# Indexer scores: the keys' low part against the queries' high part alone, two heads in the two row halves of the array

## The reference, cut to what matters

```python
s_idx = jnp.einsum('bqhd,bsd->bqhs', qi_b, ki).astype(jnp.float32)
score = jnp.einsum('bqhs,bqh->bqs', jax.nn.relu(s_idx), wi_b.astype(jnp.float32))
causal = pos[None, None, :] <= pos_b[None, :, None]
score = jnp.where(causal, score, neg)
_, sel = lax.top_k(score, topk)          # topk = 256
```

## Time and profile before

| | |
|---|---|
| median of 3 executions | 1706.78 us (1706.37 to 1708.25) |
| profiled execution, span of the core | 1702.8 us (the page gives no other time of it) |
| TensorE busy | 97% of the span, 7403 matmuls |
| VectorE, ScalarE, GpSimd busy | 51%, 34%, 25% |
| chain of work that ended last | TensorE 86%, issue 7%, VectorE 3%, ScalarE 1% |
| granted TensorE clock in the scored tiles | 1.00 of full (the 2.4 GHz level) |

### The profile page before, as it was taken

The page is one execution under the profiler, slowest core; times in us unless marked ns, Lnnn a source line. Parts: engine busy times, 40 slices in busy tenths (PEclk is TensorE's granted clock), DMA queues, the critical chain, the costliest instruction groups (busy, mean ns, idle before and its releaser), DMA issues.

```text
span 1702.8 us, 21182 instructions
## 1 busy us (share of the span) xinstructions
PE 1655.7 (97%) x7403; PEld 1323.2 (78%) x7403; DVE 862.8 (51%) x1497; ACT 584.4 (34%) x849; POOL 420.7 (25%) x285
## 2 busy tenths in 40 slices
PE   5999999999999999999999999999998899999998
PEld 4777888888888888888888888877776788888886
DVE  6326445448678777787444444467677200022003
ACT  7234444444433344432111111155555222222330
POOL 1212111112222222222222222211010344444550
PEclk8999999999999999999999999999999999999999
DMA  7411111101222222223222222222122522227322
GB/s 257 82 38 54 52 31 37 37 13 53 65 65 65 59 59 59 59 74 103 70 74 68 74 72 69 75 78 80 59 81 76 208 91 95 98 87 296 116 95 99
DMA packets 132301, 141.35 MB, mean 83 GB/s; under 512 B 8510, under 2 KB 103840, under 8 KB 129952
## 3 DMA queue, kind: packets, MB, share of 16 engines
q1 hardware_dynamic: 130720, 136.55, 25.7%
q0 software_dynamic: 1536, 4.20, 0.8%
HBM read 116.08 MB, written 24.64 MB: 83 GB/s over the span
## 4 chain that ended last, share of the span: by engine, by line
PE 86%; issue 7%; DVE 3%; ACT 1%; DMA 1%; POOL 0%; DVEq 0%; SPq 0%; ACTq 0%; POOLq 0%
PE ps L1009 18%; PE ps L1011 18%; PE ps L1010 18%; PE ps L1269 6%; PE ps L1271 6%; PE ps L1270 6%; PE ps L1096 2%; PE ps L1098 2%; PE ps L1210 2%; PE ps L1174 1%; PE ps L1187 1%; PE ps L1294 1%; PE ps L1295 1%; PE ps L1296 1%; PE ps L1194 1%
## 5 line engine op out<-in xcount | busy, mean ns | idle before, releaser
L1009 PE MATMUL ps<-hT_hi,w_lo 128*128 128x512 f32 (+1 forms) x1376 | 545.8, 397 | 0.3 <-POOL w_lo L630 0.3
L1010 PE MATMUL ps<-hT_lo,w_hi 128*128 128x512 f32 (+1 forms) x1376 | 543.8, 395 | 0.0
L1011 PE MATMUL ps<-hT_hi,w_hi 128*128 128x512 f32 (+1 forms) x1376 | 543.7, 395 | 0.0
L630 POOL TENSOR_TENSOR w_lo<-w_raw,w_hi 128x512 fp32r<-128x512 f32 (+1 forms) x172 | 236.6, 1379 | 842.2 <-ACT w_hi L711 842.2
L1011 PEld LDWEIGHTS ps<-hT_hi,w_hi 128*128 128x128 f32 (+1 forms) x1376 | 256.8, 187 | 64.4 <-issue 0.4
L1009 PEld LDWEIGHTS ps<-hT_hi,w_lo 128*128 128x128 f32 (+1 forms) x1376 | 257.1, 187 | 62.5 <-issue 2.0
L1010 PEld LDWEIGHTS ps<-hT_lo,w_hi 128*128 128x128 f32 (+1 forms) x1376 | 257.0, 187 | 60.9 <-issue 0.4
L711 ACT ACTIVATE w_hi<-w_raw 128x512 fp32r<-128x512 f32 (+1 forms) x172 | 106.6, 626 | 540.5 <-PE ps L1011 521.4
L1269 PE MATMUL ps<-wo_hi,hT_lo 128*128 128x512 f32 x448 | 178.0, 397 | 3.1 <-DVE hT_lo L1536 3.1
L1270 PE MATMUL ps<-wo_lo,hT_hi 128*128 128x512 f32 x448 | 177.7, 397 | 0.0
L1271 PE MATMUL ps<-wo_hi,hT_hi 128*128 128x512 f32 x448 | 177.6, 397 | 0.0
(11 more groups left out here) (179 smaller groups left out, 1721.6 us busy)
## 6 DMA issues: line engine op xcount, KB each, us to landing
w_raw<-in_w_in SPq DMA_DIRECT2D x168, 256.0 KB, 2.9
wo_raw<-in_w_out SPq DMA_DIRECT2D x64, 512.0 KB, 3.6
xin<-in_x SPq DMA_DIRECT2D x8, 1024.0 KB, 5.0
res<-in_x SPq DMA_DIRECT2D x8, 1024.0 KB, 9.4
out<-res SPq DMA_DIRECT2D x16, 512.0 KB, 3.9
y_lru_dram<-sg SPq DMA_DIRECT2D x8, 512.0 KB, 2.8
q_dram<-av SPq DMA_DIRECT2D x8, 512.0 KB, 3.7
gate_dram<-rg SPq DMA_DIRECT2D x8, 512.0 KB, 4.4
```

The costliest lines, as they stand in the source:

```text
L630: nc.gpsimd.tensor_tensor(w_lo[:, j, :, 0:n], w_raw[:, j, :, 0:n], w_hi[:, j, :, 0:n].bitcast(F32), ALU.subtract).then_inc(w_lo_s, 1)
L1009: nc.tensor.matmul(o, wlo, hi, start=(kt == 0), stop=False)
L1010: nc.tensor.matmul(o, whi, lo, start=False, stop=False)
L1011: return nc.tensor.matmul(o, whi, hi, start=False, stop=(kt == KT - 1))
```

## The change

A call of `score` now does both heads of one query block (a pair of units, the new `r` from 0 to 5). It first multiplies both stacks over all 128 rows by `ki_hi`, head a into `X[0]`, head b into `X[1]`. Then come the low parts of the keys, chunk by chunk, and these use only the rows that hold the queries' high part: rows 0 to 63 (`ID` is 64) of `stack_a` with `ki_lo` into `X[0]`, then rows 64 to 127 of `stack_b` with `ki_lo` into `X[1]`. The product of the two low parts is no longer computed. The count of matmuls is the same. Pairs are scored after `kt` 3, 5, 7, 9, 11 and 13. The wait on `ix_relu` is now for both units of the pair before. ScalarE and VectorE go through the units in the new order, and VectorE's second unit of a pair adds into the same block of `scores` as the first, so it waits for that one.

```diff
             def relus(t, ms):
                 for m in ms:
-                    q = FIRST_SCORED + m % (UNITS // 2)
+                    q = FIRST_SCORED + m // 2
...
-            def score(t, par, turn, ms, first=False):
...
-                    pe.wait_ge(ix_relu, k + 1)
-                    st = (stack_a, stack_b)[m // (UNITS // 2)][par]
-                    for n in range(0, w, NT):
-                        e = min(n + NT, w)
-                        nc.tensor.matmul(X[m % 2][:, n:e], st[:, q * P:(q + 1) * P], ki_lo[:, n:e],
-                                         start=True, stop=False)
-                        last = nc.tensor.matmul(X[m % 2][:, n:e], st[:, q * P:(q + 1) * P], ki_hi[:, n:e],
-                                                start=False, stop=True)
-                    last.then_inc(ix_mm, 1)
+            def score(t, par, turn, r, first=False):
...
+                pe.wait_ge(ix_relu, k + 2)
+                chunks = [(n, min(n + NT, w)) for n in range(0, w, NT)]
+                for x, st in zip(X, (stack_a[par], stack_b[par])):
+                    for n, e in chunks:
+                        nc.tensor.matmul(x[:, n:e], st[:, tok], ki_hi[:, n:e], start=True, stop=False)
+                for n, e in chunks:
+                    one = nc.tensor.matmul(X[0][:, n:e], stack_a[par][0:ID, tok], ki_lo[0:ID, n:e],
+                                           start=False, stop=True)
+                    two = nc.tensor.matmul(X[1][:, n:e], stack_b[par][ID:P, tok], ki_lo[ID:P, n:e],
+                                           start=False, stop=True)
+                one.then_inc(ix_mm, 1)
+                two.then_inc(ix_mm, 1)
...
-                project_tile(t, par, turn, between=lambda kt: score(
-                    t - 1, 1 - par, before, range(kt - 3, kt - 2) if 3 <= kt < UNITS + 3 else [], first))
+                project_tile(t, par, turn, between=lambda kt: score(t - 1, 1 - par, before, (kt - 3) // 2, first)
+                             if kt in range(3, UNITS + 3, 2) else None)
...
                     dve.wait_ge(ix_relu, k + 3)
-                    dve.wait_ge(ix_acc, k + 3)
+                    dve.wait_ge(ix_acc, k + 3 if m % 2 == 0 else k + 8)
                     acc = scores[:, off(q):off(q) + w]
-                    head = t * 2 + (m // (UNITS // 2) - 2 * T_QI)
+                    head = t * 2 + (m % 2 - 2 * T_QI)
```

More of the change, by code:

```diff
@@ L1076, in _ @@
             last.then_inc(c_var, 1)
-            def score(t, par, turn, ms, first=False):
[L1082 to L1091, removed]
-                    pe.wait_ge(ix_relu, k + 1)
-                    st = (stack_a, stack_b)[m // (UNITS // 2)][par]
-                    for n in range(0, w, NT):
-                        e = min(n + NT, w)
-                        nc.tensor.matmul(X[m % 2][:, n:e], st[:, q * P:(q + 1) * P], ki_lo[:, n:e],
-                                         start=True, stop=False)
-                        last = nc.tensor.matmul(X[m % 2][:, n:e], st[:, q * P:(q + 1) * P], ki_hi[:, n:e],
-                                                start=False, stop=True)
-                    last.then_inc(ix_mm, 1)
+            def score(t, par, turn, r, first=False):
+                q = FIRST_SCORED + r
+                w = (q + 1) * P
+                tok = slice(q * P, (q + 1) * P)
+                k = t * UNITS + (2 * r - UNITS * T_QI)
+                if r == 0:
+                    pe.wait_ge(pj_free[par], turn + 2)
+                if r == 0 and first:
+                    pe.wait_ge(ki_done, 2)
+                    pe.wait_ge(c_sd, 1)
+                    pe.wait_ge(w_nat_s, 1)
+                pe.wait_ge(ix_relu, k + 2)
[10 more added lines that the diff above has]
+                two.then_inc(ix_mm, 1)
```

## The result

The changed kernel takes 1710.27 us, median of 20 executions (1707.74 to 1713.35), against 1706.72 us for the kernel before in as many (1704.22 to 1708.91). The ratio is 1.0022, 95% interval 1.0016 to 1.0029: slower by 3.7 us (2.7 to 4.9). The forecast had the sign and the mechanism, and more than twice the size: +8.2 us. Its range, 1695 to 1721, holds the time; its likeliest case, 1709 to 1719, holds it at the low end.

What follows compares the result with a forecast made beforehand. TensorE, busy 97% of the span, was taken as the bound. Low part per tile: 1.98 + 0.66 + 2.34 = 4.98 us against 3.96, +1.02, by 8 tiles +8.2: 1706.8 becomes 1715.0 us, range 1695 to 1721.

Steps and rivals of the forecast that it cites:

- likeliest case: Whole kernel: the forecast with small variants and a bare-load rival, 1709 to 1719 us, chance 58%.
- TensorE sets the pace, the other engines have slack: Scored tiles: TensorE busy in all 30.24 us, VectorE 14.58, ScalarE 13.57; a microsecond on TensorE is one of time.
- The halves run side by side, 15.8 us saved: Low-part scoring matmuls: a pair takes the time of one, 1.98 us a tile instead of 3.96.
- Every stretch costs a break, 0.39 us: Each block's switch from 128 to 64 rows and back: 0.39 us, 2.34 us a tile, 18.7 us in all.
- rival 1: Low part in scoring: overlap without a break, -10.6 us, 1696.2 us, or 1691.0 with no late second half; chance 20%.
- Loads come one after another: Weight loads of the halves: head b's starts 0.11 us after head a's in each block, 0.66 us a tile.
- Rival 5: Two-chunk blocks: a bare load follows the first chunk, +3.5 us, 1718.5 us; counted within the forecast's 58%.
- Nothing waits for the ReLUs: Scoring's followers: two ReLUs done with 0.4 us left; first scored tile thinnest, one or two microseconds once if cover fails.
- rival 4: Scoring's followers: one is late, slack of 0.4 us fails in some pairs, 1716 to 1725 us; chance 6%.
- zero bound: Late second half in each block: lower bound of nothing, if both loads hide; total then +2.9 us.
- The signs it named: Scored tiles: period 31.2 us, first half's load about 0.3 us after the preceding matmul's start, no TensorE waits for L784.
- Time around the span: Whole kernel: median 3.98 us above the profiled span of 1702.8 us, taken as unchanged, giving span 1711.0.

Runs made afterwards that it cites:

- experiment 2: Changed kernel, but both low-part matmuls of a pair read rows 0 to 63 of `stack_a`, so no separate row halves; 1726.18 us, ratio 1.0110.
- experiment 3: Changed kernel with the low part in 128-key chunks: in halves 1721.32 us, ratio 1.0085; over all 128 rows 1733.82 us, ratio 1.0159.
- experiment 4: Changed kernel, but within each stretch all of head a's halves are written before all of head b's; 1710.61 us, ratio 1.0012.

## Why the prediction was right or wrong, step by step

- *TensorE sets the pace, the other engines have slack.* Right. The low part taken away gave back what it cost.
- *The halves run side by side, 15.8 us saved.* Right; experiment 2 gives 15.5.
- *Every stretch costs a break, 0.39 us.* Right in mechanism and size: 0.39 in the block shown, 0.40 for each stretch added or taken away. Over all six blocks the tile periods give a little less: 0.33 is -1.94 for the overlap, +0.04 for the order and six stretches of 0.37, 17.9 us in all instead of 18.7. Why the six average 0.37 and one more costs 0.40 is open. The earlier trace rows had the price, excluded the other readings, and rival 1 with them.
- *"Loads come one after another", so the second half starts 0.11 us late, 5.3 us.* **Wrong, and this is the step that failed.** The term is zero: the second half's load starts 0.01 us after the first's, and so does its matmul. From the earlier trace rows I took that fewer rows make no shorter load, which is true (a row of 0.18 us for 64 rows, 0.19 for 128), and then that two loads into different rows must queue, for which there was no row: the earlier trace rows shows queueing only between loads into the same rows. The prediction bounded this step from below with zero and gave the sum without it, +2.9 us; I then took the nearest row, though that row left out just what was new, the separate rows. The bound was the truth.
- *Rival 5, a load cannot go ahead of the matmul in its rows.* It did not happen. In the last block of the first scored tile of the changed kernel the second pair of loads starts 0.10 us after the first, while the first pair has yet to stream its 512 columns, and the second pair of matmuls then starts without a bare load:

```profile
169.49 0.49 PE L1098 MATMUL ps<-ki_lo,stack_a 64*128 64x512 f32 x1
169.59 0.19 PEld L1098 LDWEIGHTS ps<-ki_lo,stack_a 64*128 64x128 f32 x1
169.59 0.19 PEld L1100 LDWEIGHTS ps<-ki_lo,stack_b 64*128 64x128 f32 x1
169.82 0.39 PE L1098 MATMUL ps<-ki_lo,stack_a 64*128 64x512 f32 x1
```

- *Nothing waits for the ReLUs; the first scored tile is thinnest, with 0.4 us of slack.* Wrong by half a microsecond in just that place. Rows of ScalarE, VectorE and TensorE in the changed kernel there:

```profile
167.39 0.92 ACT L784 ACTIVATE relu<-ps 128x896 f32<-128x896 f32 x1 [1.42 <-DVE scores L1422]
```
```profile
164.72 1.65 DVE L1408 SCALAR_TENSOR_TENSOR c_sb<-c_sb,par_t,c_rs 128x256 f32<-128x256 f32 x2
166.29 3.33 DVE L1422 SCALAR_TENSOR_TENSOR scores<-relu,w_nat,scores 128x768 f32<-128x768 f32 x3
```
```profile
167.62 0.40 PE L1011 MATMUL ps<-hT_hi,w_hi 128*128 128x512 f32 x1
168.36 0.73 PE L1096 MATMUL ps<-ki_hi,stack_a 128*128 128x512 f32 x2 [0.34 <-ACT relu L784]
```

 Unit 9's ReLU waited for unit 7's addition behind the norm, ended at 168.31, and the sixth pair started 0.74 us after the matmul before it instead of 0.23. This is rival 4 in one pair. With it the sum comes out: eight tiles at -1.94 + 0.04 + 6*0.37, which is 0.33, are 2.6, and the first tile has 0.6 more, 3.2 us by the trace; the timing says 3.7, 2.7 to 4.9. A forecast with the zero bound would have been 1706.8 + 2.9, plus this.
- *The signs it named.* The load of the first half came 0.32 us after the start of the matmul before it (213.48 after 213.16), as forecast; the tile period of 31.2 us and the absence of any wait for L784 did not come.
- *Time around the span.* Set at 3.98 us, found 1.7. It did not enter the difference.

The 1.0 us between 1302 and 1355 us is one of the clock. Windows over that stretch, three of the changed kernel, then two of the kernel before (columns as in the earlier trace rows; the clock stands behind the engines):

```profile
1301.55:1321.78 20.23, 16.14 (x81) 11.76 (x80) 16.04 (x55) 9.81 (x22) 2.47 (x4) 1.00 0.25 82
1321.78:1325.20 3.42, 3.42 (x11) 2.42 (x10) 2.63 (x7) 1.58 (x4) 0.00 (x0) 0.50 0.28 81
1342.26:1345.68 3.42, 3.42 (x10) 2.65 (x9) 0.00 (x0) 0.00 (x0) 0.00 (x0) 0.50 0.89 371
1317.50:1335.72 18.22, 13.64 (x69) 10.31 (x68) 12.45 (x28) 9.16 (x13) 6.05 (x4) 1.00 0.19 58
1335.72:1339.13 3.41, 3.11 (x7) 2.48 (x8) 0.00 (x0) 0.00 (x0) 0.00 (x0) 0.50 0.65 219
```

In the changed kernel's profile the granted clock is at 0.50, the 1.2 GHz level, twice here, in that of the kernel before once. Ahead of the first drop TensorE had waits and was busy in 16.14 of 20.23 us (13.64 of 18.22 in the kernel before). Of the thirteen profiled executions of this case the four with 3.4 us at the lower level here pass this code in 52.3 to 52.5 us, among them the kernel before (52.35) and the kernel with ten stretches a tile (52.37); the nine with 6.8 us or more take 53.1 to 54.5 (the changed kernel 53.41). So this microsecond belongs to the execution and not to the change. What stays open is the 0.75 us ahead of the first scoring matmul, which starts anywhere from 146.5 to 151.8 us in the thirteen profiles, and the half microsecond between the 3.2 us by the trace and the 3.7 by the timing, which is inside the interval.

## What to carry to other kernels

Count the stretches, not the matmuls: work in a part of the array must save more per stretch than the 0.39 us that going there and back costs, which with 512-column matmuls of 0.233 us means two pairs or more in a row. Here four of the six blocks save less than that, 0.175 to 0.353 us. When a term's nearest row lacks just what is new about the case, the other bound deserves as much weight as that row. And when a piece of work is moved out of a slack-poor place, follow what its *end* releases, DMAs included, before calling the move free.

## What the runs showed of the hardware that I had not expected

- Loads into different row halves start within 0.01 us of each other; a pair takes 0.10 us, a single full-height load 0.11 (experiment 3).
- TensorE takes matmuls out of program order when their row halves differ (experiment 4: 0.33 us ahead, 30.61 us a tile against 31.5 by program order). The Trainium skill, "TensorE: Matmul & The Clock Gate", section "The mechanism", says that matmuls start and end strictly in program order; this trace differs, and the measurement decides. If matmuls in two halves need not keep the written order, two increments of one semaphore from the two are no proof of which half is done; no run here shows a wrong release, since the last matmuls of both halves started within 0.01 us of each other.
